# The input product of a bidirectional state space layer: four-pass fp32 to three fp32r passes with split weights

## The reference, cut to what matters

```python
def ssd_mixer(h, w_in, conv_w, conv_b, dt_bias, a_log, d_skip, norm_g, w_out):
    proj = h @ w_in                                  # 256x1024 @ 1024x8256
    z, xbc, dt_raw = jnp.split(proj, ...)            # 2048, 6144, 64 columns
    xbc = jax.nn.silu(centred_depthwise_conv(xbc, conv_w, conv_b))   # 5 taps over the tokens
    xs, b_f, c_f, b_b, c_b = jnp.split(xbc, ...)
    dt = jax.nn.softplus(dt_raw.reshape(...) + dt_bias)
    y_fwd = ssd_scan(xs, dt[:, :, 0], a[0], b_f, c_f)                # 8 groups of 4 heads
    y_bwd = flip(ssd_scan(flip(xs), flip(dt[:, :, 1]), a[1], flip(b_b), flip(c_b)))
    y = (y_fwd + y_bwd + xs * d_skip[:, None]).reshape(bsz, seqlen, SSD_D_INNER)
    y = rmsnorm_2(y * jax.nn.silu(z), norm_g)
    return y @ w_out
```

## Time and profile before

| what | value |
|---|---|
| median of the runs | 3269.51 us |
| the profiled execution | 3272.41 us |
| its span, first to last instruction | 3270.7 us |
| mean granted TensorE clock | 0.959 of full speed |
| TensorE busy in the span | 3001.6 us (92%) |
| VectorE / ScalarE / GpSimd busy | 1828.9 / 1272.1 / 297.5 us |
| the 64 quarters of this stage | 2001.7 to 2272.3 us of the span |

### The profile page before, as it was taken

The page is one execution under the profiler, slowest core; times in us unless marked ns, Lnnn a source line. Parts: engine busy times, 40 slices in busy tenths (PEclk is TensorE's granted clock), DMA queues, the critical chain, the costliest instruction groups (busy, mean ns, idle before and its releaser), DMA issues.

```text
span 3270.7 us, 42208 instructions
## 1 busy us (share of the span) xinstructions
PE 3001.6 (92%) x16936; PEld 2588.1 (79%) x16937; DVE 1828.9 (56%) x2183; ACT 1272.1 (39%) x1314; POOL 297.5 (9%) x228
## 2 busy tenths in 40 slices
PE   4978998887999999999998999999999899798998
PEld 2857996366777777777886998887899899676998
DVE  6375433965787778778554453883245344143552
ACT  1223331005666667666443441343143333123441
POOL 0005902930000000000000000012000000000000
PEclk9968999998999999999999999999999999899999
DMA  7744564035999899889563464443355456531462
GB/s 224 257 154 154 181 219 142 1 113 169 323 311 299 293 340 309 284 292 341 181 202 113 159 192 129 129 129 103 103 180 177 136 180 193 136 109 52 155 203 71
DMA packets 578794, 608.13 MB, mean 186 GB/s; under 512 B 37385, under 2 KB 533100, under 8 KB 578668
## 3 DMA queue, kind: packets, MB, share of 16 engines
q1 hardware_dynamic: 565255, 602.50, 56.9%
q10 hardware_dynamic: 13413, 3.81, 0.8%
HBM read 605.22 MB, written 1.05 MB: 185 GB/s over the span
## 4 chain that ended last, share of the span: by engine, by line
PE 80%; DVE 8%; DMA 5%; issue 3%; ACT 2%; SPq 1%; ACTq 1%; POOL 0%; DVEq 0%
PE bank L1029 24%; PE bank L899 9%; PE bank L1449 6%; PE bank L925 4%; PE bank L1350 3%; PE bank L1343 2%; PE bank L1379 2%; PE bank L1380 2%; PE bank L1347 2%; PE bank L1384 2%; DMA ring<-in_o_exp_up 2%; DMA ring<-in_o_exp_down 2%; DVE std L2589 2%; PE bank L1004 1%; PE bank L1000 1%
## 5 line engine op out<-in xcount | busy, mean ns | idle before, releaser
L2325 DVE TENSOR_TENSOR ring_r<-ring,store_area_r 128x2048 fp32r<-128x2048 f32 (+1 forms) x318 | 745.6, 2373 | 170.1 <-ACT store_area_r L1706 167.3
L1706 ACT ACTIVATE store_area_r<-ring 128x2048 fp32r<-128x2048 f32 (+1 forms) x318 | 618.8, 1975 | 194.0 <-PE bank L1029 79.2
L2688 DVE TENSOR_TENSOR ring_r<-ring,store_area_r 128x3072 fp32r<-128x3072 f32 x64 | 195.0, 3089 | 78.6 <-ACT store_area_r L2004 78.6
L1449 PE MATMUL bank<-hT,ring 128*128 128x256 f32 x1024 | 229.9, 380 | 0.0
L1029 PE MATMUL bank<-sq_r,store_area_r 128*128 128x256 f32 x1408 | 206.5, 290 | 20.9 <-ACT sq_r L1742 20.9
L899 PE MATMUL bank<-hT,ring 128*128 128x256 f32 x896 | 200.4, 385 | 25.3 <-DVE hT L2202 21.7
L899 PEld LDWEIGHTS bank<-hT,ring 128*128 128x128 f32 x896 | 172.8, 194 | 50.5 <-issue 26.5
L1449 PEld LDWEIGHTS bank<-hT,ring 128*128 128x128 f32 x1024 | 190.8, 190 | 27.1 <-issue 3.1
L1029 PEld LDWEIGHTS bank<-sq_r,store_area_r 128*128 128x128 f32 x1408 | 187.1, 195 | 25.2 <-issue 22.4
L1029 PE MATMUL bank<-sq_r,ring_r 128*128 128x256 f32 x1408 | 200.8, 286 | 0.0
L1029 PE MATMUL bank<-hT_r,store_area_r 128*128 128x256 f32 x1408 | 199.6, 285 | 0.0
(11 more groups left out here) (430 smaller groups left out, 5113.6 us busy)
## 6 DMA issues: line engine op xcount, KB each, us to landing
ring<-in_o_exp_gate SPq DMA_DIRECT2D x88, 1024.0 KB, 6.3
ring<-in_o_exp_up SPq DMA_DIRECT2D x88, 1024.0 KB, 8.9
ring<-in_ffn_w_gu SPq DMA_DIRECT2D x88, 1024.0 KB, 7.5
ring<-in_o_exp_down SPq DMA_DIRECT2D x32, 1536.0 KB, 8.1
ring<-in_ffn_w_down SPq DMA_DIRECT2D x32, 1408.0 KB, 8.8
ring<-in_o_exp_down SPq DMA_DIRECT2D x32, 1280.0 KB, 10.9
ring<-in_ssd_w_in SPq DMA_DIRECT2D x32, 1024.0 KB, 6.9
ring<-in_e_mod_mix_w SPq DMA_DIRECT2D x12, 1024.0 KB, 11.6
```

What stands on the lines that cost most here:

```text
L1449: ins = mm(dense_bank(i, s)[:, half * T:(half + 1) * T], slot(u, s, KD)[:, k, half * P:(half + 1) * P], h(k), start=(k == 0), stop=(k == K ...
L1706: activation(dst, slot(u, s, kk), ACT.Copy).then_inc(w_high, 1)
L2325: nc.vector.tensor_tensor(slot(u, s, kk, rounded=True), slot(u, s, kk), as_f(high), ALU.subtract).then_inc(w_low, 1)
L2688: vec.tensor_tensor(down_wide(u, rounded=True)[:, j:j + m, :], down_wide(u)[:, j:j + m, :], as_f(down_high_wide(i)[:, j:j + m, :]), ALU.su ...
```

## The change

All 16 units of the stage take three fp32r passes instead of one fp32 product. The dt unit stays as it is. For each unit i, ScalarE copies both slots to fp32r high parts (slot 0 to the unused ends of the ring's slots, slot 1 to `act_r` and the end of `store_area_r`; one buffer each). VectorE writes slot 0's low part in place, GpSimd slot 1's, in two instructions (6 and 2 blocks: 128x1536 and 128x512). ScalarE also copies `hT` to a high part, VectorE writes its low part over `hT` once the dt product is done. In the orders: ScalarE makes the two high parts of unit 0 inside the norm, ahead of the root; later slot 0's at t % 4 == 2 after `high_used`, slot 1's at t % 4 == 0 after the unit before is done and ahead of `unit_out`. VectorE writes slot 0's low part at t % 4 == 3, ahead of the taps of that t. GpSimd walks over t, with `low_parts(t // 4)` at t % 4 == 1 and `weights(g)` at step 5. A half slot is now 24 products.

```diff
+    def ssd_high_parts(s):
+        if s == 0:
+            return [(slice(0, KD), ring_r[:, 0:4, 8 * COLS:10 * COLS].rearrange("p n f -> p n f"))]
+        return [(slice(0, 6), act_r[:, 16:22, :]), (slice(6, KD), high_area(83, 2))]
+    def ssd_slot(u, s, rows, rounded=False):
+        r = (ring_r if rounded else ring)[:, 2 * u.r + s, rows.start * COLS:rows.stop * COLS]
+        return r.rearrange("p (n f) -> p n f", f=(2 if s == 0 else 1) * COLS)
...
@@ GpSimd, ssd
-                for g in range(6):
-                    weights(g)
-                gates(0)
-                weights(6)
-                gates(1)
-                weights(7)
-                gates(2)
+                def low_parts(i):
+                    u = Unit(base["ssd_in"] + 1 + i)
+                    pool.wait_ge(ssd_high, 2 * i + 2)
+                    for rows, high in ssd_high_parts(1):
+                        out, w = ssd_slot(u, 1, rows, rounded=True), ssd_slot(u, 1, rows)
+                        ins = nc.gpsimd.tensor_tensor(out, w, as_f(high), ALU.subtract)
+                    ins.then_inc(pool_low, 1)
+                for t in range(QUARTERS):
+                    if t % 4 == 1:
+                        low_parts(t // 4)
+                    for g, step in scan_steps(t):
+                        if step == 5:
+                            weights(g)
+                    if t >= 53 and t % 4 == 1:
+                        gates((t - 53) // 4)
                 gates(3)
@@ TensorE, quarter(t)
+                    out, cols = dense_bank(i, s)[:, half * T:(half + 1) * T], slice(half * P, (half + 1) * P)
                     if half == 0:
-                        pe.wait_ge(slot_full[2 * u.r + s], u.full())
+                        pe.wait_ge(ssd_high, 2 * i + s + 1)
                     for k in range(KD):
-                        ins = mm(dense_bank(i, s)[:, half * T:(half + 1) * T], slot(u, s, KD)[:, k, half * P:(half + 1) * P], h(k),
-                                 start=(k == 0), stop=(k == KD - 1))
-                    if s == half == 1:
-                        ins.then_inc(unit_done, 1)
+                        if t == 0:
+                            pe.wait_ge(h_high, parts_before("ssd_in") + k + 1)
+                        mm(out, ssd_high_block(s, k, cols), ssd_h_high(k), start=(k == 0), stop=False)
+                    if half == 0:
+                        pe.wait_ge((ssd_low, pool_low)[s], i + 1)
+                    for k in range(KD):
+                        mm(out, slot(u, s, KD, rounded=True)[:, k, cols], ssd_h_high(k), start=False, stop=False)
+                    for k in range(KD):
+                        if t == 0:
+                            pe.wait_ge(h_low, parts_before("ssd_in") + k + 1)
+                        ins = mm(out, ssd_high_block(s, k, cols), h_lo[:, k, :], start=False, stop=(k == KD - 1))
+                    if half == 1:
+                        ins.then_inc(unit_done if s else high_used, 1)
@@ ScalarE, ssd
+                def high_parts(i, s):
+                    u = Unit(first + 1 + i)
+                    se.wait_ge(slot_full[2 * u.r + s], u.full())
+                    for rows, high in ssd_high_parts(s):
+                        ins = activation(high, ssd_slot(u, s, rows), ACT.Copy)
+                    ins.then_inc(ssd_high, 1)
+                norm("mix_0", meanwhile=lambda: [high_parts(0, s) for s in range(2)])
+                for k in range(KD):
+                    se.wait_ge(h_ready, KD * H_BEFORE["mix_0"] + k + 1)
+                    activation(ssd_h_high(k), hT[:, k, :], ACT.Copy).then_inc(h_high, 1)
...
-                for t in range(4, QUARTERS + 1):
+                for t in range(2, QUARTERS + 1):
                     for g, step in scan_steps(t):
                         scan(g, step)
+                    if t % 4 == 2 and t < QUARTERS - 4:
+                        se.wait_ge(high_used, EVEN_USED + t // 4 + 1)
+                        high_parts(t // 4 + 1, 0)
                     if t % 4 == 0:
                         i = t // 4 - 1
+                        if t < QUARTERS:
+                            se.wait_ge(unit_done, Unit(first + 1 + i).at(1))
+                            high_parts(i + 1, 1)
                         unit_out(i)
@@ VectorE, ssd
+                def low_parts(i):
+                    u = Unit(first + 1 + i)
+                    ve.wait_ge(ssd_high, 2 * i + 1)
+                    for rows, high in ssd_high_parts(0):
+                        vec.tensor_tensor(ssd_slot(u, 0, rows, rounded=True), ssd_slot(u, 0, rows), as_f(high),
+                                          ALU.subtract).then_inc(ssd_low, 1)
+                low_parts(0)
+                ve.wait_ge(unit_done, Unit(first).at(1))
+                for k in range(KD):
+                    ve.wait_ge(h_high, parts_before("ssd_in") + k + 1)
+                    vec.tensor_tensor(h_lo[:, k, :], hT[:, k, :], as_f(ssd_h_high(k)), ALU.subtract).then_inc(h_low, 1)
...
-                for t in range(4, QUARTERS):
+                for t in range(2, QUARTERS):
                     if t == DT_AT:
                         columns()
                     for g, step in scan_steps(t):
                         scan(g, step)
+                    if t % 4 == 3 and t < QUARTERS - 4:
+                        low_parts(t // 4 + 1)
                     i, part = t // 4 - 1, t % 4
-                    if SSD_UNITS[i][0] == "conv":
+                    if i >= 0 and SSD_UNITS[i][0] == "conv":
                         taps(i, part)
```

More of the change, by code:

```diff
@@ L169, in program @@
     gate_x = sem("gate_x")
-    gate_w = sem("gate_w")
+    ssd_high, ssd_low, pool_low = sem("ssd_high"), sem("ssd_low"), sem("pool_low")
     decay_ps, decay_x, soft_ready = sem("decay_ps"), sem("decay_x"), sem("soft_ready")
-    cum_ready = sem("cum_ready")
     key_raw, key_exp, key_ready, key_used = sem("key_raw"), sem("key_exp"), sem("key_ready"), sem("key_used")
@@ L413, in scan_steps, with ssd_high_block, ssd_h_high @@
         return [divmod(at, STEPS)] if at >= 0 and at < 8 * STEPS else []
+    def ssd_high_parts(s):
+        if s == 0:
+            return [(slice(0, KD), ring_r[:, 0:4, 8 * COLS:10 * COLS].rearrange("p n f -> p n f"))]
+        return [(slice(0, 6), act_r[:, 16:22, :]), (slice(6, KD), high_area(83, 2))]
+    def ssd_high_block(s, k, cols):
+        if s == 0:
+            at = (8 + k % 2) * COLS
+            return ring_r[:, k // 2, at + cols.start:at + cols.stop]
+        return act_r[:, 16 + k, cols] if k < 6 else high_area(83, 2)[:, k - 6, cols]
+    def ssd_slot(u, s, rows, rounded=False):
+        r = (ring_r if rounded else ring)[:, 2 * u.r + s, rows.start * COLS:rows.stop * COLS]
+        return r.rearrange("p (n f) -> p n f", f=(2 if s == 0 else 1) * COLS)
+    def ssd_h_high(k):
+        n, at = (k, 10) if k < 4 else (4 + (k - 4) // 2, 8 + (k - 4) % 2)
+        return ring_r[:, n, at * COLS:(at + 1) * COLS]
     dense_bank = lambda i, s: banks[2 * (i % 2) + s]
@@ L520, in program, with parts_before @@
     EVEN_H = KD if has("even_ffn") else 0
+    EVEN_USED = GU_UNITS if has("even_ffn") else 0
+    SPLIT_INPUT = [s for s in stages if s in SPLIT or s == "ssd_in"]
+    def parts_before(stage):
+        return EVEN_H + KD * SPLIT_INPUT.index(stage)
     def slots_before(stage, i):
@@ L1034, in h_parts @@
                     if p == 0:
-                        pe.wait_ge(h_high, EVEN_H + KD * n + k + 1)
+                        pe.wait_ge(h_high, parts_before(stage) + k + 1)
                     if p == 2:
-                        pe.wait_ge(h_low, EVEN_H + KD * n + k + 1)
+                        pe.wait_ge(h_low, parts_before(stage) + k + 1)
                 def gate_up(u, i):
@@ L2012, in ssd @@
             def ssd():
-                norm("mix_0")
                 first = base["ssd_in"]
+                def high_parts(i, s):
[8 more added lines that the diff above has]
+                    activation(ssd_h_high(k), hT[:, k, :], ACT.Copy).then_inc(h_high, 1)
                 se.wait_ge(cols_in, 16 * (len(COL_LOADS) + 3))
@@ L2359, in ffn @@
                 for k in range(KD):
-                    ve.wait_ge(h_high, EVEN_H + KD * n + k + 1)
+                    ve.wait_ge(h_high, parts_before(stage) + k + 1)
                     nc.vector.tensor_tensor(h_lo[:, k, :], hT[:, k, :], as_f(h_hi[:, k, :]), ALU.subtract).then_inc(h_low, 1)
```

4 lines of the change are left out of this document (2 added, 2 removed).

## The result

| | median of the runs | profiled execution | its span | granted clock |
|---|---|---|---|---|
| after | 3317.76 us (4 runs, 3313.53 to 3332.35) | 3313.53 us | 3311.5 us | 0.954 |
| before, alongside | 3271.47 us (4 runs, 3269.17 to 3282.57) | - | - | - |

The ratio is 1.0146, 95% interval 1.013 to 1.0161: slower by 43 to 53 us. The prediction said 3313 us, range 3280 to 3341, with 0.91 on slower.

The account below looks back on a forecast made before the run. TensorE bounds the kernel now; VectorE, held by GpSimd, was to become the bound. From the 3269.5 us median, 9 (start) + 40.2 (quarters 16 to 51) - 5.7 (quarters 52 to 63) = +43.5 gave 3313 us, range 3280 to 3341.

Parts of the forecast that it names:

- From its arrival on, VectorE stood through the whole of the other's instruction: VectorE's taps beside GpSimd instructions: VectorE stands still throughout, 3.19 of 3.61 us in one case.
- GpSimd's price: GpSimd's low part per unit: 3.45 us for 128x1536 plus 1.27 us for 128x512, 4.7 us.
- TensorE's rate: Each quarter becomes 24 products of 0.122 us, 2.93 us instead of 3.45, gaining 0.52 us.
- Quarters 16 to 51: Three periods of 12 quarters take 200.5 us against 160.3: a loss of 40.2 us, ends 10 and 60.
- 67.4 us: VectorE's 12-quarter period: 47.1 own work, 21.1 GpSimd, 1.2 handovers, less 2 credited; 54.3 us before.
- TensorE waits for it at one place, pass 2 of the first quarter of each unit: In the scan, TensorE waits for VectorE's low part, queued behind 15 of 20 taps; some 6 us per unit.
- The start: Up to quarter 16: late root, reciprocal and dt product, then VectorE's list, make it 9 us late; ends 5 and 12.
- The 1.4 us for the clock: Before quarter 0: 1.4 us added because TensorE's clock would stay low for longer after idling.
- some 5: Idle time in us read from a profile row, after which the clock was still 0.52 eight microseconds on.
- No taps are left: Quarters 52 to 63: VectorE has slack, so 6.3 us gained less 0.6 for small waits, -5.7; ends -6.3 and +3.
- GpSimd hardly holds anyone: Quarters 52 to 63: GpSimd's instructions were expected to cause almost no standstill.
- rival A: Same mechanism, milder, bank readers lying in GpSimd's shadow: period 57.4 us, kernel 3278 to 3283 us; chance 10%.

Follow-up runs that it names:

- e1: The changed kernel with GpSimd's subtraction cut from 128x2048 to 128x64 per unit, slot 1's middle pass rereading its high part: 3266.6 us, ratio 0.997 to before.
- e2: The changed kernel with slot 1's low parts made by VectorE instead of GpSimd: 3287.1 us, ratio 1.0042 to the kernel before.
- e5: The kernel before plus unread GpSimd subtractions (128x1536, 128x512) per unit, two different inputs, started after the banks' copy: 3297.0 us, ratio 1.0086.
- e4: The kernel before plus unread GpSimd subtractions (128x1536, 128x512) per unit, one tensor as both inputs, started at the unit's end: 3276.7 us, ratio 1.0009.
- e3: The changed kernel with VectorE's slot 0 subtraction cut to 128x64, the middle pass rereading the high part: 3310.8 us, ratio 1.0107 to before.
- v4: The kernel before with three split passes only for the four gate units (quarters 48 to 63), all low parts on VectorE: 3266.5 us, ratio 0.9977.

## Why the prediction was right, and where it was not

**The mechanism was right.** "From its arrival on, VectorE stood through the whole of the other's instruction", read from four rows, is what e1 (-51 us), e2 (-31 us) and e5 (+27 us on the kernel before) show. e4 sets its limit: the same kind of work costs nothing that can be told when it starts while VectorE waits or reads banks. GpSimd's price (4.7 us taken, 3.59 + 1.36 median with its own waits) and TensorE's rate (0.96 us per eight products, 0.120 each) came as put. ScalarE's longer list is not the cause by itself: e1 keeps all of it and loses nothing.

**Quarters 16 to 51: near in size, wrong in form.** +34.0 against +40.2, inside its ends. The two later periods took 68.1 and 69.3 us against the 67.4 of the sum; the whole overshoot is the first, 56.8 where the prediction has 67.4 - 1.7 = 65.7. The step that failed is "67.4 us" as a sum of VectorE's list. In the periods that it meets, VectorE is idle for 5.6 and 5.8 us, and e3 took 6.9 us of each period out of the list for 3.1 and 4.4. The period is the loop above. That the list's sum comes near it, because both contain the same holds, is argued and not shown, so its match to 1 or 2 us counts as luck in part. "TensorE waits for it at one place, pass 2 of the first quarter of each unit" was wrong here: 5.0 of 41.7 us. It waits at step 1 of a group: 15.8 us for a silu behind the taps of the unit before, 16.1 us for a bank that VectorE empties late, two deadlines that the prediction never listed. Before quarter 16, where there are no steps, the place was right: 7.7 us there, and e3's 10.0.

**The start: +6.3 against +9.** Root and reciprocal came late as worked out: the dt product +3.8 against +4.4, 2.9 of it by the root and 0.9 by the scaling of x, which GpSimd's second piece held. The 1.4 us for the clock did not come: the dt product took 7.92 us at a granted clock of 0.78 in both kernels, after 6.77 us of waiting as after 2.96. One of the rows behind the 1.4 was misread as well: TensorE had stood 7.04 us before the one at 2360 us, not "some 5".

```profile
1995.30:2003.30 8.00, 7.97 (x33) 3.72 (x34) 4.87 (x9) 4.89 (x13) 0.00 (x0) 0.78 0.01 2
```

**Quarters 52 to 63: +3.2 against -5.7, just outside its end of +3.** The failed step is "No taps are left". The last five, of t = 51, are still in VectorE's queue when quarter 52 starts, and four GpSimd instructions of two lines fall on them:

```profile
2258.12 8.29 DVE L2888 SCALAR_TENSOR_TENSOR store_area<-silu_g,vc,store_area 128x256 f32<-128x256 f32 x5
2258.35 3.57 POOL L878 TENSOR_TENSOR ring_r<-ring,act_r 128x1536 fp32r<-128x1536 f32 x1 [2.31 <-ACT store_area_r L2066]
...
2261.89 1.44 POOL L878 TENSOR_TENSOR ring_r<-ring,store_area_r 128x512 fp32r<-128x512 f32 x1
2263.29 2.84 POOL L871 TENSOR_TENSOR store_area<-store_area,act 128x512 f32<-128x512 f32 x2
...
2268.35 0.77 PE L1522 MATMUL bank<-store_area 128*128 128x128 f32 x2 [7.92 <-DVE std L2913]
```

2.2 us of taps take 8.29, TensorE stands 7.9 us, and then the granted clock is 0.50:

```profile
2266.00:2269.00 3.00, 0.65 (x3) 0.69 (x4) 2.98 (x8) 1.06 (x1) 0.13 (x1) 0.50 0.00 0
```

Of the 9.5 us between +3.2 and the 6.3 us that the passes save, this wait is 7.9; the slow start behind it can hold the rest. The last GpSimd row belongs to `gates(0)`, old work that meets new work: the prediction counted "GpSimd hardly holds anyone" from the rows of the kernel before, where that neighbour was absent.

**The sum** was right because -6.2 and -2.7 stood against +8.9. The range starts at 3280 us, inside rival A's 3278 to 3283, which it was said to take in.

**What stays open.** How the loop's 68 us divide between the hold, the clock and ScalarE's order was not separated, nor why the first period is ten microseconds shorter than the others. Nor was the hold tried against the same GpSimd work with its output or inputs elsewhere. e1 and e3 leave out most of a low part, so their results are not the layer's; of the other kernels v4 is the fastest, and its gain, 5 us in the trace to the end of the scan and 4 to 11 us by the interval, is small.

## What to carry to other kernels

An idle engine is not free if it shares something with the full one: before moving work to GpSimd, read in the timeline what VectorE's instructions take beside GpSimd's own, and charge the whole length wherever the two would be due together; where GpSimd can start while the other waits or reads banks, it can cost nearly nothing (e4). A busy share of 94% does not make a list that can be summed, even where the sum comes out: ask which consumer's deadline comes first, and whether removing an item moves it. A cheaper pass paid here only in the stretch where the engine that feeds it has slack, so split by stretch, not by stage.

## What the runs showed of the hardware

- GpSimd subtracts 128x1536 in 3.44 us from two different tensors and in 2.75 us where both inputs are the same tensor (128x512: 1.27 and 1.04), in e5 and e4.
- GpSimd writes fp32r at its fp32 pace: 128x1536 took 3.42 us at least in after, 3.43 in fp32 in e5.
- The hold goes both ways: GpSimd's 128x512 subtraction took 3.32 us when VectorE's 128x2048 one had started first, and each of several short taps can be held anew by the next GpSimd instruction (7.85 us for four that take 1.38).
- The dt product took 7.92 us after 3.0 and after 6.8 us of idle TensorE, at a granted clock of 0.78 both times.
